# Weight tiles loaded two at a time: 2 MB transfers into a ring of two pairs instead of 1 MB transfers into a ring of four tiles

## The reference

```python
h = rmsnorm(x)                                  # (512, 2048)
q, k, v, og, gkf, gkb, glu, ga, gb = split(h @ w_in)
o  = gla_forward(q, k, v, gkf) + gla_backward(q, k, v, gkb)   # 4 heads
ya = (rmsnorm(o) * silu(og)) @ gla_w_o
u  = depthwise_conv31(glu_a * sigmoid(glu_b))
yb = silu(layernorm(u)) @ conv_w_pw2
x  = x + (sigmoid(ga) * ya + sigmoid(gb) * yb) @ w_out
h2 = rmsnorm(x)
s  = keys . (h2 @ peer_w_q)                     # 8 heads, 2 halves, 128 keys
idx, gate = top16_of_products(s)                # 16 expert rows per head and token
act = gelu(h2 . u_tab[idx])                     # 16 dot products of 2048
x  = x + sum(gate * act * v_tab[idx])
out = rmsnorm(x)
```

## Time and profile before

| | |
|---|---|
| median of 3 runs | 4347.53 us (4343.13 to 4353.24) |
| profiled execution, its own time | 4345.06 us |
| span of its instructions | 4343.2 us |
| TensorE busy | 3741.6 us, 86% |
| VectorE busy | 2644.4 us, 61% |
| DMA, all queues | 1531.06 MB, mean 353 GB/s |
| of these the gathers (q0) | 1073.77 MB |

### The profile page before, as it was taken

The page is one execution under the profiler, slowest core; times in us unless marked ns, Lnnn a source line. Parts: engine busy times, 40 slices in busy tenths (PEclk is TensorE's granted clock), DMA queues, the critical chain, the costliest instruction groups (busy, mean ns, idle before and its releaser), DMA issues. The chain is left out here.

```text
span 4343.2 us, 39659 instructions
## 1 busy us (share of the span) xinstructions
PE 3741.6 (86%) x13716; PEld 2254.6 (52%) x13716; DVE 2644.4 (61%) x3888; ACT 887.6 (20%) x2061; POOL 773.3 (18%) x525
## 2 busy tenths in 40 slices
PE   9999999999999999767699698758888887777777
PEld 3444489446666667663688586334444442322222
DVE  3232258103899999765777867886666664544444
ACT  2233210101112112242111111122222222212112
POOL 0000000000133232232221311222111121212111
PEclk9999999999999999888899899879999999999999
DMA  3111148888899999999999999999999999999998
GB/s 139 62 59 58 69 175 300 300 316 307 317 367 380 385 412 415 393 406 410 426 426 426 422 417 426 426 389 427 413 428 428 428 419 428 423 428 428 427 428 367
DMA packets 142779, 1531.06 MB, mean 353 GB/s; under 512 B 15312, under 2 KB 21584, under 8 KB 22096
## 3 DMA queue, kind: packets, MB, share of 16 engines
q0 software_dynamic: 73728, 1073.77, 58.9%
q1 hardware_dynamic: 67248, 445.32, 26.5%
q10 hardware_dynamic: 1696, 10.62, 0.6%
HBM read 1525.46 MB, written 4.19 MB: 352 GB/s over the span
## 5 line engine op out<-in xcount | busy, mean ns | idle before, releaser
L1725 PE MATMUL bank<-arena_h,wring 128*128 128x128 f32 (+5 forms) x6656 | 1395.7, 373 | 135.8 <-DVE arena_h L1440 41.9
L1725 PEld LDWEIGHTS bank<-arena_h,wring 128*128 128x128 f32 x6656 | 1033.3, 197 | 494.6 <-issue 187.1
L619 POOL DMA_INDIRECT arena_c<-in_peer_uv,arena_c x256 | 509.4, 1990 | 2509.3 <-DVE arena_o L1372 1372.3
L1363 DVE SCALAR_TENSOR_TENSOR arena_c<-arena_c 128x2048 f32<-128x2048 f32 x256 | 586.2, 2290 | 185.4 <-DMA arena_c<-in_peer_uv,arena_c 185.2
L2116 PE MATMUL bank<-arena_c,arena_h 128*128 128x512 f32 x1024 | 479.0, 612 | 156.5 <-ACT arena_h L991 156.5
L1372 DVE SCALAR_TENSOR_TENSOR arena_o<-arena_c,arena_o 128x2048 f32<-128x2048 f32 x234 | 550.1, 2351 | 71.9 <-ACT arena_c L799 65.4
L2083 PE MATMUL bank<-arena_c,cols 128*128 128x512 f32 x1024 | 471.3, 604 | 93.0 <-ACT cols L949 91.1
L1636 DVE SCALAR_TENSOR_TENSOR arena_c<-arena_c 128x2048 f32<-128x2048 f32 x128 | 293.5, 2293 | 333.5 <-DMA arena_c<-in_peer_uv,arena_c 333.3
L797 ACT ACTIVATE arena_c<-arena_c 128x1 f32<-128x1 f32 x384 | 78.0, 203 | 1909.7 <-DVE arena_c L1363 1419.2
L632 POOL DMA_INDIRECT arena_c<-in_peer_uv,arena_c x256 | 261.7, 1022 | 1033.7 <-PE bank L2083 522.8
L1582 DVE SCALAR_TENSOR_TENSOR arena_c<-arena_c 128x2048 f32<-128x2048 f32 x128 | 293.4, 2293 | 238.4 <-DMA arena_c<-in_peer_uv,arena_c 237.4
(11 more groups left out here) (228 smaller groups left out, 2629.5 us busy)
## 6 DMA issues: line engine op xcount, KB each, us to landing
wring<-in_w_in SPq DMA_DIRECT2D x176, 1024.0 KB
wring<-in_w_out SPq DMA_DIRECT2D x48, 1024.0 KB
wring<-in_peer_w_q SPq DMA_DIRECT2D x48, 1024.0 KB
wring<-in_gla_w_o SPq DMA_DIRECT2D x32, 1024.0 KB
wring<-in_conv_w_pw SPq DMA_DIRECT2D x32, 1024.0 KB
wring<-in_w_v SPq DMA_DIRECT2D x16, 1024.0 KB
wring<-in_w_ga SPq DMA_DIRECT2D x16, 1024.0 KB
wring<-in_w_o_quarters SPq DMA_DIRECT2D x16, 1024.0 KB
```

What stands on the lines that cost most here:

```text
L619: pool.indirect_dma_start(out=slot_of(n), out_offset=None, in_=uv_tab, in_offset=at)\
L1363: V.scalar_tensor_tensor(row, row, 1.0, block_of(h2, n // P), ALU.mult, ALU.mult, accum_out=act_u[:, n % TOP:n % TOP + 1]).then_inc(dotted, 1)
L1725: last = M(ps[bank][:, at:at + hi - lo], w_tile(slot)[:, k, :], act_in[:, k, lo:hi], start=k == 0, stop=k == KT - 1)
```

## The change

Two neighbouring tiles of a matrix are now stored together on the host (`in_pairs`): per partition the 8192 bytes of the first tile and behind them the 8192 bytes of the second. One transfer brings both, 2 MB with 16384 bytes a partition, into two neighbouring slots of the ring. The ring has the same size and TensorE uses the same tiles in the same order.

```diff
-        w_in_slot = [sem(f"w_slot{s}") for s in range(RING)]
+        w_in_pair = [sem(f"w_pair{s}") for s in range(RING // 2)]
...
-        def slot_all(n):
+        def slot_pair(n):
 
-            return wring[:, (n % RING) * TILE:(n % RING + 1) * TILE]
+            return wring[:, (n % RING) * TILE:(n % RING + 2) * TILE]
...
-            def load(n, i, per, src):
+            def load_pair(n, i, per, src):
 
-                hold(sp, w_used, i * per + (n + 1), sp_passed)
-                sp.dma_start(slot_all(n), src).then_inc(w_in_slot[n % RING], 16)
+                hold(sp, w_used, i * per + (n + 2), sp_passed)
+                sp.dma_start(slot_pair(n), src).then_inc(w_in_pair[n % RING // 2], 16)
 
             def loads(n, i, per, w, at, count):
 
-                for m in range(count):
-                    load(n + m, i, per, piece(w, at + m))
+                for m in range(count // 2):
+                    load_pair(n + 2 * m, i, per, piece(w, at + m))
...
                 with sp.Fori(0, KT // 4) as i:
-                    loads(first, i, 8, w_gate, i * 4, 4)
-                    loads(first + 4, i, 8, w_val, i * 4, 4)
+                    loads(first, i, 8, w_gate, i * 2, 4)
+                    loads(first + 4, i, 8, w_val, i * 2, 4)
...
                 if i is None:
-                    pe.wait_ge(w_in_slot[n % RING], 16 * (n // RING + 1))
+                    pe.wait_ge(w_in_pair[n % RING // 2], 16 * (n // RING + 1))
...
+def in_pairs(tiles):
+
+    n, p, f = tiles.shape
+    return np.ascontiguousarray(tiles.reshape(n // 2, 2, p, f).transpose(0, 2, 1, 3)).reshape(n // 2, p, 2 * f)
```

More of the change, by code:

```diff
@@ L518, in _ @@
                 sp.dma_start(hT[:, 4 * c:4 * c + 4, :], x_t[:, 4 * c:4 * c + 4, :]).then_inc(x_in[c], 16)
-            def load(n, i, per, src):
-                hold(sp, w_used, i * per + (n + 1), sp_passed)
-                sp.dma_start(slot_all(n), src).then_inc(w_in_slot[n % RING], 16)
+            def load_pair(n, i, per, src):
+                hold(sp, w_used, i * per + (n + 2), sp_passed)
+                sp.dma_start(slot_pair(n), src).then_inc(w_in_pair[n % RING // 2], 16)
             def loads(n, i, per, w, at, count):
-                for m in range(count):
-                    load(n + m, i, per, piece(w, at + m))
+                for m in range(count // 2):
+                    load_pair(n + 2 * m, i, per, piece(w, at + m))
             with sp.Fori(0, HEADS) as h:
-                loads(0, h, HEAD_TILES, w_in, h * 2 + WQ, 2)
-                loads(2, h, HEAD_TILES, w_in, h * 2 + WK, 2)
-                loads(4, h, HEAD_TILES, w_v, h * 4, 4)
+                loads(0, h, HEAD_TILES, w_in, h + WQ // 2, 2)
+                loads(2, h, HEAD_TILES, w_in, h + WK // 2, 2)
+                loads(4, h, HEAD_TILES, w_v, h * 2, 4)
             def pair_loads(first, w_gate, o_gate, w_val, o_val):
                 with sp.Fori(0, KT // 2) as i:
-                    loads(first, i, 4, w_gate, i * 2 + o_gate, 2)
-                    loads(first + 2, i, 4, w_val, i * 2 + o_val, 2)
+                    loads(first, i, 4, w_gate, i + o_gate // 2, 2)
+                    loads(first + 2, i, 4, w_val, i + o_val // 2, 2)
             def row_loads(first, w, o):
                 with sp.Fori(0, KT // 4) as i:
-                    loads(first, i, 4, w, i * 4 + o, 4)
+                    loads(first, i, 4, w, i * 2 + o // 2, 4)
             pair_loads(SB_GLU0, w_in, WGATE, w_in, WGLU)
@@ L555, in _ @@
             row_loads(SB_WQ0, w_q, 0)
-            loads(SB_GLU1, 0, 4, w_in, WGATE, 2)
-            loads(SB_GLU1 + 2, 0, 4, w_in, WGLU, 2)
+            loads(SB_GLU1, 0, 4, w_in, WGATE // 2, 2)
+            loads(SB_GLU1 + 2, 0, 4, w_in, WGLU // 2, 2)
             with sp.Fori(0, 4) as j:
-                loads(SB_OG1, j, 8, w_in, j * 4 + WOG, 4)
-                loads(SB_OG1 + 4, j, 8, w_in, j * 2 + (WGATE + 2), 2)
-                loads(SB_OG1 + 6, j, 8, w_in, j * 2 + (WGLU + 2), 2)
+                loads(SB_OG1, j, 8, w_in, j * 2 + WOG // 2, 4)
+                loads(SB_OG1 + 4, j, 8, w_in, j + (WGATE // 2 + 1), 2)
+                loads(SB_OG1 + 6, j, 8, w_in, j + (WGLU // 2 + 1), 2)
             with sp.Fori(0, 3) as j:
                 for a in range(2):
[L565 to L568, removed]
+                    loads(SB_MA1 + 4 * a, j, 12, w_in, j * 2 + (WGA // 2 + a), 2)
+                    loads(SB_MA1 + 4 * a + 2, j, 12, w_o, j * 2 + a, 2)
+                loads(SB_MA1 + 8, j, 12, w_in, j + (WGATE // 2 + 5), 2)
+                loads(SB_MA1 + 10, j, 12, w_in, j + (WGLU // 2 + 5), 2)
             for a in range(2):
-                loads(SB_MA1_LAST + 4 * a, 0, 8, w_in, WGA + 12 + 2 * a, 2)
-                loads(SB_MA1_LAST + 4 * a + 2, 0, 8, w_o, 12 + 2 * a, 2)
+                loads(SB_MA1_LAST + 4 * a, 0, 8, w_in, WGA // 2 + 6 + a, 2)
+                loads(SB_MA1_LAST + 4 * a + 2, 0, 8, w_o, 6 + a, 2)
             row_loads(SB_GB1, w_in, WGB)
@@ L1687, in tile_ready @@
                 if i is None:
-                    pe.wait_ge(w_in_slot[n % RING], 16 * (n // RING + 1))
+                    pe.wait_ge(w_in_pair[n % RING // 2], 16 * (n // RING + 1))
                 else:
-                    pe.wait_ge(w_in_slot[n % RING], i * (16 // RING * per) + 16 * (n // RING + 1))
+                    pe.wait_ge(w_in_pair[n % RING // 2], i * (16 // RING * per) + 16 * (n // RING + 1))
             pe.sem_inc(w_used, RING - 1)
@@ L2131 @@
         "gla_w_o", "w_o_quarters", "conv_w_pw2", "w_pw2_quarters", "w_out", "norm2_g", "peer_w_q", "peer_keys", "peer_uv", "final_norm_g"]
+def in_pairs(tiles):
+    n, p, f = tiles.shape
+    return np.ascontiguousarray(tiles.reshape(n // 2, 2, p, f).transpose(0, 2, 1, 3)).reshape(n // 2, p, 2 * f)
 def in_tiles(w):
     n = w.shape[1] // P
-    return np.ascontiguousarray(w.reshape(KT, P, n, P).transpose(2, 1, 0, 3)).reshape(n, P, KT * P)
+    return in_pairs(w.reshape(KT, P, n, P).transpose(2, 1, 0, 3).reshape(n, P, KT * P))
 def in_quarters(w):
     n = w.shape[1] // 512
-    return np.ascontiguousarray(w.reshape(4, QUART, P, n, 512).transpose(3, 0, 2, 1, 4)).reshape(4 * n, P, QUART * 512)
+    return in_pairs(w.reshape(4, QUART, P, n, 512).transpose(3, 0, 2, 1, 4).reshape(4 * n, P, QUART * 512))
 def laid_out(inputs):
```

## The result

The changed kernel takes 4634.31 us (median; 4623.62 to 4635.96) against 4348.93 of the kernel before on the same chip: ratio 1.0661, 95% interval 1.0648 to 1.0673. The forecast was 4440 us and slower; the direction is right, the size is off by 194 us. The profiled execution spans 4633.3 us, 290.1 more than before.

The account below looks back on a forecast made before the run. TensorE was taken to delay the first gather, after which a full DMA sets the end. 4345.1 + 85 (before the gathers) + 8 (after) - 3 (larger packets) + 3 (clock) = 4438 profiled, 4440 us median; range 4410 to 4465, chance 0.63.

Parts of the forecast that it names:

- What bounds the kernel: Whole kernel: TensorE sets when gathers start; afterwards the full DMA, 423 us-mean GB/s over 2090 to 4325 us, sets the end.
- That gives a least period of 8.8 us ... Sum +85 us: Before the first gather: a pair takes at least 8.8 us against 6.87 in merged branches and output projection; +85 us altogether.
- I take 7.3 ... with bounds 6.9 and 7.5: Before the first gather: 2 MB, with the DMA otherwise idle, lands 7.3 us after its issue; bounds 6.9 and 7.5.
- The lag: Merged branches: time from a tile's first matmul to the next transfer's issue, 1.27 us with 512 columns moving.
- +3: Clock term: TensorE pausing 2 us in every 8.8 may at times get 1.2 instead of 2.4 GHz; +3 us, bound +10.
- The query tiles: Block 0's 16 query tiles: a pair already takes 9.5 us, more than the least period of 8.2, so no cost.
- +8, bounds -20 and +40: After the first gather, 1720 to 2090 us: late pairs less what the weights' larger share gives back; +8 us.
- DMA traffic that falls clearly in this stretch: Sign that the prediction is wrong: DMA traffic between 1485 and 2090 us falling clearly under what it is now.
- if a third of them meet an empty gather queue, 8 x 1.5 = 12 us: 1720 to 2090 us: of 24 pairs a third find no gathers queued and come 1.5 us late each, 12 us.
- the wait spreads: Rival, 4465 to 4520 us: shallower lookahead costs 25 to 70 us more between 1485 and 2090 us; chance 0.17.
- a pair in under 14 us: Block 1's query projection: 16384-byte packets give weights half the full DMA, 213 GB/s, so a pair takes under 14 us.
- The rival of packets staying at 8192 bytes: Rival, 4480 to 4530 us: transfers are cut in two, weights keep a third, a contended pair takes 17.9 us; chance 0.06.

Follow-up runs that it names:

- joint wait: Kernel before, with a pair's two 1 MB transfers issued together two tiles ahead and its first tile waiting for both: 4650.81 us, ratio 1.0686.
- own waits: Kernel before, with a pair's two 1 MB transfers issued together two tiles ahead, each tile waiting only for its own: 4389.07 us, ratio 1.0111.

## Why the prediction was wrong

**What bounds the kernel: right.** The first gather came 161 us later and all of it reached the end (the kernel with pairs for block 0 only: first wait +157, total +169). From the first tile of blocks 2 and 3 to the end the two kernels need 2133 and 2134 us. One reading was loose: from about 2090 us on the earlier trace rows has 389 to 428 GB/s, not 426 to 428; the sums use the mean of 423.

**"That gives a least period of 8.8 us ... Sum +85 us": the mechanism right, a term too small.** TensorE waits at every second tile in block 0, as said, but the period is 10.0 us and the sum 161. The step that failed is the landing, "I take 7.3 ... with bounds 6.9 and 7.5". It measures 8.4 from issue to start, where the forecast had 7.3 + 0.2: 0.9 us in each of the 64 pairs of block 0 before the query tiles, some 58 of the 76 us. I had extrapolated from megabytes that follow each other as separate transfers of 8 KB runs, and for those it is right: two transfers take 7.5, and the kernel built of them loses 97 us, near the 85. One transfer of 2 MB in 16 KB runs is not two of 1 MB in 8 KB runs. The lag was sized right at full clock (1.38 for 1.27), but behind many of the new waits the clock was granted at 1.2 GHz; the mean lag is 1.65 us. "+3" was meant for both parts, and here alone it is some 15 us (0.38 us in 40 pairs). The range could not hold this: its upper bound for landing was 7.5.

The query tiles were put at nothing, "more than the least period of 8.2". TensorE waits 15.3 us for their weights after the first gathers, and they take 94 us for 76. The forecast priced their pairs by a landing with the DMA otherwise idle, but the last of them land beside the first gathers.

**"+8, bounds -20 and +40" behind the first gather: wrong.** It is 108 us, 815 against 707, and 100 without the late start. The forecast had named the sign of it, DMA traffic that falls clearly in this stretch: 360 GB/s against 411. Two steps failed. The first is the count, "if a third of them meet an empty gather queue, 8 x 1.5 = 12 us". The second is the bounds of the region: the sum has no term for 1485 to 1720 us, and TensorE was expected to gain a little in the query projection behind 2090. The stretch in three pieces, the kernel before and then the changed one; the last two pieces are about the region that the forecast counted:

```profile
1485.00:1721.00 236.00, 218.17 (x1186) 168.66 (x1186) 230.88 (x290) 47.99 (x95) 70.43 (x29) 0.96 1.00 414
1721.00:1895.00 174.00, 120.19 (x839) 106.99 (x838) 136.43 (x138) 60.19 (x108) 52.04 (x21) 0.85 0.96 393
1895.00:2082.00 187.00, 132.78 (x659) 95.88 (x658) 110.63 (x96) 46.35 (x83) 54.96 (x22) 0.85 1.00 416
...
1666.00:1939.00 273.00, 228.98 (x1154) 176.45 (x1153) 227.79 (x287) 46.56 (x93) 69.79 (x28) 0.91 0.90 359
1939.00:2130.00 191.00, 124.52 (x831) 111.30 (x829) 135.49 (x139) 60.47 (x108) 50.53 (x20) 0.83 0.88 345
2130.00:2359.00 229.00, 149.72 (x660) 105.43 (x660) 109.91 (x94) 47.02 (x84) 53.43 (x22) 0.78 0.85 338
```

They lose 37, 17 and 42 us, and the query projection behind them 12 more (122 for 110). I compared with a tile period of 7.38 us, read where the DMA is full all the time, and took it for the stretch before too. My account of the difference, argued from the waits and the DMA share and not tested by a run of its own: the gathers come at VectorE's pace, the DMA moves 411 GB/s but the queues are not both full at every moment, and TensorE's bursts of fast tiles are served by three transfers in flight. With one pair in flight TensorE waits for it, then VectorE waits for TensorE, the slots fill, and the DMA has only the one pair to do. What the runs show is the part of the joint wait: this stretch takes 739 us with own waits and 831 with the joint wait. The waits of the changed kernel in that stretch (1666 to 2481 us):

```profile
PE bank L1725 <- DMA wring<-in_w_in: 50.9, 12, 9.4
PE bank L1725 <- DMA wring<-in_gla_w_o: 31.5, 8, 6.2
PE bank L1878 <- DMA wring<-in_w_out: 30.7, 8, 6.6
...
DVE arena_o L1488 <- PE bank L1878: 66.1, 4, 19.6
DVE arena_c L1428 <- PE bank L1725: 47.4, 7, 8.2
DVE arena_c L1384 <- PE bank L1725: 28.0, 3, 9.3
```

Against the earlier trace rows TensorE's wait for the output weights went from 13.4 to 30.7 us, VectorE's for TensorE from 38.8 to 66.1 and from 32.5 to 47.4. The rival "the wait spreads" named this mechanism and this place, and priced it at 25 to 70 us; from 1485 to 2082 us it is 37 + 17 + 42 = 96.

**The shares: the direction right, the size not.** The forecast had a pair land in 12.3 us in full contention and TensorE gain 0.5 us a tile, "a pair in under 14 us" in block 1's query projection. There a pair takes 15.5 us where two tiles took 14.75, so TensorE lost; in the kernel with pairs after block 0 the median landing there is 14.0 us. By the forecast's own working (2.4 us fixed, the rest at the share of the weights) that is 2.1 MB / 11.6 us = 181 GB/s, an estimate, between the third that it had before and the half that was forecast. That the longer runs do raise the share is shown by the 17.2 us with 8 KB runs. In blocks 2 and 3 the stretch to the last output projection is 716 us for 726, at 414 against 418 GB/s, but nothing of it reaches the end (2134 for 2133). The kernels with 8 KB runs and joint waits need 762 and 782 there. The rival of packets staying at 8192 bytes is excluded by q1's count.

**The formula for one DMA.** The Trainium skill ("DMA: Bandwidth & Descriptors", anatomy of one DMA) gives 6.8 us for 2 MB by its fit for GpSimd's path. The traces have 8.3 us from issue to landing on SyncE's queue. The measurement decides, and the formula was further off than the extrapolation.

**What stays open.** Why one transfer of 2 MB takes 0.5 to 0.6 us longer than two of 1 MB issued together, and why the longer runs add 0.3 to 0.4. The packet records say where it is not: in the merged branches of three kernels (one transfer of 16 KB runs, one of 8 KB runs, two of 8 KB runs) the first packet starts 1.0 us after the issue, and the last one ends 0.4 to 0.5 us before TensorE starts (medians). It ends 8.0, 7.6 and 7.0 us after the issue. So the difference lies between the first packet and the last, although a packet of 8 KB takes 309 ns in both kernels that have it, and one of 16 KB 611: the DMA engines stand still for longer between packets. No run had more ring slots with pairs, so that a larger ring would take the loss away is not shown.

## What to carry to other kernels

A larger transfer into the same ring is first of all a coarser ring: count what is in flight and how late the last useful moment of the issue is, before counting bytes per packet. Here the joint wait cost 262 us, and the longer runs gave back some 70 (840 to 815 us and 762 to 716), all of it where gathers ran beside the weights; price a landing from a transfer of that very size, not by adding smaller ones. And a rate read where everything is full does not price the stretch in which three engines wait for each other in turn: here even one single tile less ahead cost 67 us (4412.95 against 4345.76), 10 of them before the first gather.

## What the runs showed of the hardware

A transfer onto partitions 0 to 63, followed by one onto 64 to 127, runs at little more than half of the rate; the same bytes on even and odd partitions do not. Stages of block 0 with no gathers, and below each one microsecond of it with a pair in flight, the halves first, then odd and even:

```profile
1000.00:1200.00 200.00, 128.59 (x222) 52.66 (x221) 2.08 (x3) 1.79 (x3) 0.00 (x0) 0.78 0.68 147
1003.00:1004.00 1.00, 1.00 (x2) 0.33 (x1) 0.00 (x0) 0.00 (x0) 0.00 (x0) 0.50 1.14 262
```

```profile
805.00:950.00 145.00, 117.45 (x255) 48.72 (x254) 6.51 (x10) 12.81 (x24) 0.00 (x0) 0.96 0.62 232
866.00:867.00 1.00, 1.00 (x4) 0.52 (x3) 0.00 (x0) 0.00 (x0) 0.00 (x0) 1.00 0.97 410
```

262 GB/s against 410 in flight, and 147 against 232 over the stages at nearly the same DMA share (0.68 and 0.62): a packet of 16384 bytes took 1285 ns with the halves and 611 with odd and even rows (medians). While gathers ran beside the halves, from 3000 to 3400 us, the whole DMA moved only 256 GB/s at a share of 0.94. The Trainium skill ("SBUF — State Buffer", the section on the DMA port swizzle) says that partitions 0 to 63 reach 8 of 16 ports; the trace agrees, with the rates above.
